# Modulation rows by four column strips at a time, and new places for the pieces of the rounds

## The reference, cut to what matters

```python
cond = jax.nn.silu(c)
for l in range(DEPTH):                      # DEPTH = 2, D_MODEL = 1024
    mod = cond @ ada_w[l] + ada_b[l]        # [1, 1024] @ [1024, 3072]
    shift, scale, gate = jnp.split(mod, 3, axis=-1)
    h = rms_norm(x, norm_g[l]) * (1.0 + scale[:, None, :]) + shift[:, None, :]
    ...                                     # layer 0: z = h @ even_w_in, conv, rwkv7; layer 1: attention
    x = x + gate[:, None, :] * out
```

## Time and profile before

| | us |
|---|---|
| median of 3 runs | 3179.05 (3177.11 to 3180.06) |
| the profiled execution | 3180.33 |
| its span | 3178.5 |
| PE busy in it | 3062.0 (96%) |
| DVE busy | 2134.2 (67%) |
| ACT busy | 1237.4 (39%) |
| POOL busy | 861.5 (27%) |
| share of PE in the chain that ended last | 76% |

### The profile page before, as it was taken

The page is one execution under the profiler, slowest core; times in us unless marked ns, Lnnn a source line. Parts: engine busy times, 40 slices in busy tenths (PEclk is TensorE's granted clock), DMA queues, the critical chain, the costliest instruction groups (busy, mean ns, idle before and its releaser), DMA issues.

```text
span 3178.5 us, 38156 instructions
## 1 busy us (share of the span) xinstructions
PE 3062.0 (96%) x15318; PEld 2417.5 (76%) x15318; DVE 2134.2 (67%) x3453; ACT 1237.4 (39%) x1768; POOL 861.5 (27%) x550
## 2 busy tenths in 40 slices
PE   8889999999999999999999999999999999999997
PEld 4567777677777666878887788878888888888886
DVE  3678888768789766484989899466665444444445
ACT  3334444335333655324333466533223222233224
POOL 2233433222344210143455422322222110111100
PEclk9899999999999999999999999999999999999998
DMA  7221111334222111333244467766554333343341
GB/s 258 86 77 47 54 47 57 113 115 165 70 85 73 41 40 40 111 95 93 83 140 133 142 211 238 240 214 201 187 193 147 112 120 126 119 126 120 113 133 53
DMA packets 167568, 382.91 MB, mean 120 GB/s; under 512 B 10848, under 2 KB 77408, under 8 KB 167264
## 3 DMA queue, kind: packets, MB, share of 16 engines
q1 hardware_dynamic: 167392, 380.48, 37.3%
HBM read 320.14 MB, written 60.29 MB: 120 GB/s over the span
## 4 chain that ended last, share of the span: by engine, by line
PE 76%; DVE 15%; ACT 5%; POOL 2%; DMA 2%; issue 1%; SPq 0%; DVEq 0%; ACTq 0%; POOLq 0%
PE ps L738 21%; PE ps L740 20%; PE ps L739 20%; DVE oh L2409 2%; PE ps L1143 2%; DVE at L2147 2%; PE ps L1071 2%; DVE ai L2145 1%; PE ps L910 1%; PE ps L930 1%; PE ps L1051 1%; POOL wsp L2510 1%; PE ps L884 1%; POOL pk L2626 1%; DVE at L2135 1%
## 5 line engine op out<-in xcount | busy, mean ns | idle before, releaser
L738 PE MATMUL ps<-hT,wsp 128*128 128x512 f32 x2016 | 826.8, 410 | 39.5 <-POOL wsp L2510 27.4
L2510 POOL TENSOR_TENSOR wsp<-ring,wsp 128x1024 fp32r<-128x1024 f32 x207 | 513.9, 2486 | 1068.4 <-ACT wsp L1198 1032.6
L740 PE MATMUL ps<-hT,wsp 128*128 128x512 f32 x2016 | 792.5, 393 | 0.0
L739 PE MATMUL ps<-hT,wsp 128*128 128x512 f32 x2016 | 791.6, 393 | 0.0
L738 PEld LDWEIGHTS ps<-hT,wsp 128*128 128x128 f32 x2016 | 381.9, 189 | 146.3 <-issue 23.0
L740 PEld LDWEIGHTS ps<-hT,wsp 128*128 128x128 f32 x2016 | 381.8, 189 | 82.8
L739 PEld LDWEIGHTS ps<-hT,wsp 128*128 128x128 f32 x2016 | 382.8, 190 | 80.4 <-issue 8.6
L2633 POOL TENSOR_TENSOR ex<-ex 128x512 fp32r<-128x512 f32 x128 | 176.0, 1390 | 831.4 <-ACT ex L1593 831.4
L1198 ACT ACTIVATE wsp<-ring 128x1024 fp32r<-128x1024 f32 x311 | 321.9, 1051 | 97.1 <-PE ps L740 81.1
L2433 DVE TENSOR_TENSOR xT<-ps,xT 128x512 f32<-128x512 f32 x256 | 174.6, 687 | 260.5 <-PE ps L740 260.5
L738 PE MATMUL ps<-ex 128*128 128x512 f32 x808 | 314.8, 390 | 2.0 <-DVE ex L1653 2.0
(11 more groups left out here) (407 smaller groups left out, 4773.9 us busy)
## 6 DMA issues: line engine op xcount, KB each, us to landing
ring<-in_eu SPq DMA_DIRECT2D x128, 512.0 KB, 3.6
ring<-in_ev SPq DMA_DIRECT2D x128, 512.0 KB, 3.6
gd<-oh SPq DMA_DIRECT2D x8, 4096.0 KB, 14.9
ex<-gd SPq DMA_DIRECT2D x32, 1024.0 KB, 6.7
ring<-in_ein SPq DMA_DIRECT2D x57, 512.0 KB, 3.7
ring<-in_oin SPq DMA_DIRECT2D x39, 512.0 KB, 3.6
ex<-zd SPq DMA_DIRECT2D x17, 1024.0 KB, 9.1
ring<-in_ada SPq DMA_DIRECT2D x30, 512.0 KB, 3.6
```

The lines of the kernel that those rows point to most:

```text
L738: pe.matmul(out, W[0], R[0], start=first, stop=False)
L739: pe.matmul(out, W[0], R[1], start=False, stop=False)
L740: return pe.matmul(out, W[1], R[0], start=False, stop=last)
L2510: pool.tensor_tensor(s[:, 1, :], raw_of(i), s[:, 0, :].bitcast(F32), ALU.subtract).then_inc(pool_done, G.step("lo", i))
```

## The change: four products for two loads, and a new table

At an even kp, PE only opens the bank and goes on; at an odd kp it waits for both units and issues the four products, blocks 0 to 3 or 4 to 7, one on each strip. Each unit is still marked as used by itself, after its second matmul.

```diff
                     w.wait_ge(*free)
                     w.wait_ge(scalar_done, A("cond"))
                     w.wait_ge(vector_done, V("clear"))
+                if kp % 2 == 0:
+                    return
                 out = dense.at["row", l, g]
-                w.wait_ge(*landed(n))
-                for i in range(2):
-                    k = 2 * kp + i
-                    p = 32 * (k % 4)
-                    r = pe.matmul(out[p:p + 1, :], cond[:, k:k + 1], raw_of(n)[:, i * 512:(i + 1) * 512], start=k < 4, stop=k >= 4)
-                r.then_inc(tensor_done, T.step("use", n))
+                for u in (n - 1, n):
+                    w.wait_ge(*landed(u))
+                for u in (n - 1, n):
+                    for i in range(2):
+                        k = 2 * (kp + u - n) + i
+                        p = 32 * (k % 4)
+                        r = pe.matmul(out[p:p + 1, :], cond[:, k:k + 1], raw_of(u)[:, i * 512:(i + 1) * 512], start=k < 4, stop=k >= 4)
+                    r.then_inc(tensor_done, T.step("use", u))
```

All eleven lists of `PLACES` have new numbers. One of them, for the group of pieces that round 0 lays in:

```diff
-    "first": (303, 346, 351, 359, 425, 425, 513, 523, 523, 523, 523, 523, 523, 810, 863, 872, 882),
+    "first": (368, 416, 416, 426, 465, 485, 518, 528, 528, 528, 528, 528, 528, 800, 888, 893, 893),
```

More of the change, by code:

```diff
@@ L40 @@
 PLACES = {
-    "first": (303, 346, 351, 359, 425, 425, 513, 523, 523, 523, 523, 523, 523, 810, 863, 872, 882),
[L42 to L46, removed]
[11 rows of a table removed]
+    "first": (368, 416, 416, 426, 465, 485, 518, 528, 528, 528, 528, 528, 528, 800, 888, 893, 893),
+    "prep": (416, 437, 442, 476, 489, 546, 600, 631, 665, 745, 833, 833, 833, 928, 949, 979, 1005),
+    "invert": (0, 26, 65, 101, 149, 213, 279, 298, 342, 385, 425, 459, 516, 519, 578, 626, 652, 700, 761, 817,
+        880, 918, 918, 949, 955),
+    "solve": (81, 176, 193, 325, 354, 426, 456, 477, 506, 598, 682, 746, 768, 791, 806, 911, 911, 933, 958, 958),
+    "conv": (3, 81, 92, 96, 126, 126, 138, 167, 175, 175, 175, 191, 271, 271, 281, 281, 291, 367, 369, 377, 377,
[11 rows of a table added]
 }
```

## The result

| | median | runs |
|---|---|---|
| before | 3178.69 us | 5, 3177.11 to 3180.06 |
| after | 3194.83 us | 5, 3190.55 to 3198.85 |

The ratio after/before is 1.0052, 95% interval 1.0038 to 1.0067: about 16 us slower. The forecast was 3175.5 us, the range ended at 3182.0, and slower had a chance of 0.05. The forecast was wrong in sign.

A forecast was written before the change was run, and what follows sets the result against it. PE, busy 96% of the span, was taken as the bound. Gains of 0.7 (round 0), 0.8 (round 7), 1.0 (round 8) and 1.1 us (round 9) sum to 3.6, giving 3175.5 against the median of 3179.05; range 3168.0 to 3182.0.

The forecast's parts named there:

- The places in the steady rounds: Rounds 1 to 6: the new table leaves both PE waits as they were; 0 each, within 0.3 us either way.
- Rival 4: New places open waits, 1 us in each of six rounds (3181.5, chance 0.08), or close both old ones (3167.7, 0.07).
- Round 7: Six groups, later ones waiting for loads; the dense piece starts at 628.1, not 628.88: gain 0.8 us.
- The ring's part: Each group waits for the first load into slots freed together: at least 4.65 us from group start to group start.
- rival 3: Slow clock after new waits: two stretches of 1.7 us in rounds 0 and 7, 3178.9 us, chance 0.08.
- Round 0: At row (0, 4) PE newly waits 2.7 us for DVE, later loads are asked for earlier: gain 0.7 us.
- Round 1: PE waits about 2.7 us for unit 38, covered by DVE's and POOL's queue: 0, up to +1.6 us.
- Round 8: Three groups of products become two, with time between them for loads: gain 1.0 us.
- Round 9: `lnv` comes about 2 us later, so its wait of 1.1 us goes: gain 1.1 us.
- First 40 us: Nothing changes: PE waits for other work, and its products already stand side by side or in idle time.
- The rest: Behind round 9 nothing is tied to absolute times, so what is won is kept.
- Rival 2: Second load lands late, the ring holds PE: slower if first loads exceed 4.2 us; +4.7, 3183.8 us, chance 0.10.

The follow-up runs named there:

- new_conv_old: The changed kernel with the whole list of convolution taps set back to its old places; ratio 1.0005 to the kernel before, median 3182.95 us.
- three_old: The changed kernel with only taps 9 to 11 set back to places 222, 226 and 266; ratio 1.0007 to the kernel before, median 3186.51 us.
- old_taps_early: The kernel before with only taps 7 to 11 moved ahead of the state update; ratio 1.0012 to the kernel before, median 3187.80 us.
- pair_only: The grouped products of the changed kernel with the old table of places; ratio 1.0042 to the kernel before, median 3195.22 us.
- eight_new: The kernel before with only the six new lists of places for rounds 8 and 9; ratio 1.0000 to the kernel before, median 3179.67 us.
- places_only: The single products of the kernel before with the new table of places; ratio 1.0035 to the kernel before, median 3194.43 us.
- pair_l0: The kernel before, old places, with grouped products only for the six rows of layer 0; ratio 1.0027 to the kernel before, median 3189.17 us.
- behind_st: The changed kernel with taps 8 to 11 at place 194, directly behind the state update; ratio 1.0018 to the kernel before, median 3188.37 us.
- pair_l1: The kernel before, old places, with grouped products only for the five rows of layer 1; ratio 1.0012 to the kernel before, median 3185.67 us.

## Why the prediction was wrong

1. **The places in the steady rounds: 0 within 0.3 us, measured 1.0 to 1.6 us a round at full clock.** This is the step that failed. It read: "Both waits of the earlier trace rows come from pieces whose neighbours stay as they were, so they stay." They did stay. But I looked only at the order on PE and at the two waits that existed, and asked nowhere which of DVE's instructions a tap now stands ahead of. Three taps of 0.78 us more ahead of the state update moved it by 2.4 us against the masked copies, to where it takes 1.80 and not 0.56 us. Rival 4 had this outcome (1 us in each round, 3181.5) with 0.08, with no mechanism behind it. The order of DVE around `st` would have shown it, and POOL's low part at 291.74 was in the trace of before, and so was an update of 1.20 us beside such a part. Once in each of five rounds, this makes some 6 of the 16 us.
2. **Round 7: -0.8, measured +3.9.** The ring's part was sized well: groups 4.7 and 4.9 us apart (4.65), and with the taps' list set back the stage is 0.7 us shorter than before. What failed is the path ahead of the second group: PE waits 2.4 us for a state update that stands behind taps, which is the same missed question, though the port plays no part here. At full clock that costs 1.4 us (27.3 in new_conv_old to 28.7 in three_old); the other 3.2 up to 31.9 come with the clock of 0.89. That is rival 3, once: a slow stretch behind a new wait, where the sum had counted on as many slow stretches as before. Behind the waits of 1.4, 0.6 and 1.3 us for loads the products were at full speed.
3. **Round 0: -0.7, measured -4.9.** The new wait (2.67 us for 2.7) and the dense piece's start were right. The gain on top goes with the clock, and it is not shown to be the change's: new_conv_old, with the same order in round 0 as after, took 114.4 us, and old_taps_early, with the order of before, 110.5.
4. **Round 1: 0, measured +1.9.** The wait for unit 38 was 0.8 us, not 2.7. pair_only, with the old places, had 2.7 there; its round was 0.3 us longer. After, `p2` waits for DVE's `p1` copy for 2.2 us in this stage, before for 0.9. The stage also holds the first update of 1.80 us (at 219.8). With the old list of taps it is 76.8 us, as before, so the growth comes with that list too.
5. **Round 8: -1.0, measured -1.6.** The number is near by luck. I had put it down to two groups in place of three; but single products at the new places have it too (71.6 us in eight_new, 70.3 in places_only), and groups at the old places make the round longer (75.0). It comes from the places.
6. **Round 9: -1.1, measured -0.1 up to `gn2`.** The wait for `lnv` did go, but the wait of L738 for L1958 (L1954 before) grew from 1.3 to 1.9, and one of 1.0 us for the state update came.
7. **First 40 us: 0, measured +3.7.** "Its products already stand side by side or in idle time" holds for PE's work, but not for the loads: waits before those products on the early buffers rose from 5.7 to 9.1 us. With round 0 the stretch is 1.2 us shorter than before, though, within what equal orders differ by.
8. **The rest** is 3.8 us longer, and why isn't shown. Over all runs it was between 2429.5 us (pair_l0) and 2437.9 (behind_st), 2431.7 in pair_only, so much of it can be what one execution differs from another by. But the six runs with ten or eleven new lists lie at 2434.3 to 2437.9, and those with old places at 2429.5 to 2435.3, so a part may be the places' own. A part may go with the clock: the traces' granted clock is at half for 34 us of this stage in pair_l0 and pair_l1 (2429.5 and 2429.6 us), for 44 before, 48 after and 51 in behind_st (the last 25 us left out). It stays open.

Rival 2 (the second load holds PE up, and it is slower) is what pair_only shows, by 1.0042, but not by its condition: loads over 4.2 us. They took 3.57 and 3.71 us in the chain of after. I had costed it from the places that the groups were given; with the old ones four waits of 5.7 us in sum open in round 7 alone. Its prices were also summed too high: by the prediction's own steps, loads of 4.2 us make round 7 later by 0.7 us, not 1.1, and loads of 5.0 us by 3.2, not 3.7.

## What to carry to other kernels

When a table moves work that nobody waits for, list for each engine which instruction that others wait for it now stands ahead of, and which instructions of the engine that shares its ports run at the new time. Grouping operations that each free a slot of a short ring saves issue time on the busy engine and spends it on loads: here, with the old places, 8.5 us saved and 18.3 us of waits. And try the two halves of a change apart before believing a sum of small gains. Two terms that I had worked out row by row came true within 0.3 us (the new wait of round 0, the distance of the groups in round 7). Others did not, and the term that I set to 0 decided.

## What the runs showed of the hardware

- One DVE instruction of 128x128 elements with two inputs in SBUF took 0.35 us alone, 0.56 beside a short POOL copy and 1.80 when it started 0.73 or 0.74 us into POOL's 128x1024 low part, in all five steady rounds. In round 9 it started 1.32 us into one, and took 1.20. A tap of 128x512 with one input in PSUM took 0.79 us beside the same POOL instruction, and as much without it.
- Eight records of products on four strips, both loads there, took 1.04 us at full clock and 1.82 to 1.88 us in three of the 14 groups, at half clock.
- In the same order of work the granted clock of a stretch differs by kernel and execution: from 100 to 125 us 0.86 and 0.97 (before, old_taps_early), from 40 to 152 us 0.89 and 0.97 (new_conv_old, after), and in the first 40 us between 0.83 and 0.96. A single execution's gain of 4 us in round 0 is no evidence.
- The same wait of 2.4 us in round 7 was followed by a stretch at half clock in after, and by none in three_old; the stages took 31.9 and 28.7 us.
